# A macaron decoder layer on one core: split weights of two k tiles woven in SBUF in the first feed-forward chunk of both layers

## The chip, the core and the metric

The kernel runs on one core of a Trainium2 chip. Its time is the device time of one execution in microseconds, as the median of several; three runs of the kernel before gave 2042.21 us (2042.13 to 2042.24). One more execution was taken by the hardware profiler, and every row below comes from that one. Matmuls run on TensorE (PE, with its weight loads as PEld), the rounding of weights on ScalarE (ACT), the subtractions on VectorE (DVE), and the loads are issued by SyncE (SP).

## The reference

Everything is float32, x is 256 x 2048. A SwiGLU feed-forward layer stands before and after a block of two token mixers:

```python
x = x + 0.5 * swiglu(rmsnorm(x, ffn1_norm[l]), ffn1_w_gate[l], ffn1_w_up[l], ffn1_w_down[l])
...                      # dilated attention and forgetting attention, merged by two gates
x = x + 0.5 * swiglu(rmsnorm(x, ffn2_norm[l]), ffn2_w_gate[l], ffn2_w_up[l], ffn2_w_down[l])
return rmsnorm(x, final_norm)

def swiglu(x, w_gate, w_up, w_down):
    return (jax.nn.silu(x @ w_gate) * (x @ w_up)) @ w_down
```

`w_gate` and `w_up` are 2048 x 5632, `w_down` is 5632 x 2048. "Both layers" in this text are the two feed-forward layers.

## The kernel before

**Products in three matmuls.** Each factor of a product is split into a rounded high part (type fp32r) and a rest, the low part, that is rounded too. A product is hi x hi + hi x lo + lo x hi, three matmuls into one PSUM bank. The tokens (x transposed, `xT_hi`, `xT_lo`) are the stationary operand of 128 x 128, the weights are the moving operand of 128 x 512.

**Slabs.** Weights come in loads of 1 MB: four k tiles of 128 rows by 512 columns, in one of the four slots of `raw`. A slab is half a load, two k tiles. ACT rounds a slab (`round_slab`, one instruction of 128 x 1024 elements) into `w_hi` or `more_hi`; DVE subtracts that from the raw half (`split_slab`, one instruction of the same size) and puts the rest into `w_lo` or `more_lo`; then PE multiplies it. `w_hi` and `w_lo` hold slots 0 to 3 of a ring of six in the feed-forward layers, `more_hi` and `more_lo` slots 4 and 5. In a slot k tile 0 has the first 512 columns, k tile 1 the next 512.

**A first chunk.** The 5632 hidden columns are worked in 11 chunks of 512. The first chunk of each layer is written out: 16 slabs, 8 of the gate weights (offsets 0 to 7), then 8 of the up weights (offsets 8 to 15). A slab is multiplied by `slab`, called by `wide`: for both k tiles (j) and both halves of the tokens (t) three matmuls, twelve in all. In layer 1 slabs 0 to 3 are multiplied by `first_wide` instead. The ten chunks that follow use a scheme of seven products per block (`product`) and are not concerned. Before and in the first chunk x is still being transposed, scaled (`scale_tokens` on DVE, or on ACT in layer 1) and split (`round_x`, `split_x`) chunk by chunk; PE waits for a chunk of x ahead of every even slab.

**What orders the work.** The program of every engine is written out in order. ACT waits for the load (`raw_landed`) and, once the ring is full, for PE to be done with the slab that held the slot (`slab_done`). DVE waits for ACT (`hi_ready`), PE for DVE (`lo_ready`). SP loads into a slot of `raw` when DVE has subtracted the slab that was there (`lo_ready`). DVE has other work between its splits: sums of token pairs (`sum_pairs`, `split_pairs`) for the chunks that follow, the scaling of x and the mean for the norm.

The central lines of `slab` are 765 to 767, in `round_slab` 1343, in `split_slab` 1749; 1356 and 1788 are the same steps for the chunks that follow.

Of the kernel before, what the change touches and what calls it, by code (L numbers as in the profile page):

```python
# [19 lines left out]
F32 = mybir.dt.float32  # L20
F32R = mybir.dt.float32r
BF16 = mybir.dt.bfloat16
ALU = mybir.AluOpType
ACT = mybir.ActivationFunctionType
# [4 lines left out]
TT = SEQ // P  # L29
# [23 lines left out]
WIDE, HALF_W, DOWN = 8, 4, 8  # L53

FIRST, STEP = 2 * WIDE, 33
# [43 lines left out]
FFN_START = (0, FFN2)  # L99
# [74 lines left out]
class Place:  # L174
# [13 lines left out]
    def slab(self, offset):  # L188
        n = self.start + offset
        return n if self.i is None else self.i * self.per + n  # L190
# [11 lines left out]
def mix_place(start, per=0, i=None):  # L202
    return Place(start, FFN_LOADS + (DIL_LOADS + (start - MERGE) // 2 if start >= MERGE else 0), per, per // 2, i)


def dil_place(c):
    return Place(MIX + D_FIRST[c], FFN_LOADS + c * D_LOADS)


def dil_slab(e):  # L210

    c = max(c for c in range(D_PAIRS) if D_FIRST[c] <= e)
    r = e - D_FIRST[c]
    for s, (first, group, loads) in enumerate(D_SEVEN[c]):
        if first <= r < first + PAIR_SLABS:
            return c, r, ("paired", s, r - first)
    for first, group, l in D_GATE[c] + D_UP[c]:
        if first <= r < first + 2:
            return c, r, ("direct", l, r - first)
# [25 lines left out]
def build(nc, x, ffn1_norm, ffn1_w_gate, ffn1_w_up, ffn1_w_down, mix_norm, w_in, b_forget,  # L245
# [127 lines left out]
    ps = nc.alloc_psum_tensor("ps", [P, 8, CH], F32)  # L373
# [11 lines left out]
    def slot_hi(place, offset):  # L385
        s = place.slot(offset)
        return w_hi[:, s] if s < MIX_RING else more_hi[:, s - MIX_RING]

    def slot_lo(place, offset):
        s = place.slot(offset)  # L390
        return w_lo[:, s] if s < MIX_RING else more_lo[:, s - MIX_RING]

    def raw_half(place, offset):
        return raw[:, offset // 2 % LOADS, offset % 2 * 2:offset % 2 * 2 + 2, :]

# [53 lines left out]
    def sem(name):  # L449
        return nc.alloc_semaphore(name)  # L450
# [33 lines left out]
    hi_ready = sem("hi_ready")  # L484
    lo_ready = sem("lo_ready")
    slab_done = sem("slab_done")
# [92 lines left out]
    def fox_turn(c, r):  # L579

        if F_PAIR <= c < D_PAIRS - 1 and r in FOX_Q_TURNS:
            return c, 0, FOX_Q_TURNS.index(r)
        if F_PAIR < c and r in FOX_K_TURNS:
            return c - 1, 1, FOX_K_TURNS.index(r)
        return None
# [9 lines left out]
    with block:  # L595
# [133 lines left out]
        def tokens(t):  # L729
            return slice(t * P, (t + 1) * P)  # L730
# [21 lines left out]
        def _(pe):  # L752
# [4 lines left out]
            def slab(place, offset, banks, lhs, k0, first, last):  # L757

                hi_w, lo_w = slot_hi(place, offset), slot_lo(place, offset)
                pe.wait_ge(lo_ready, place.slab(offset + 1))  # L760
                for j in range(2):
                    for t in range(TT):
                        hi, lo = lhs(k0 + j, t)
                        acc = ps[:, banks[t], :]
                        nc.tensor.matmul(acc, hi, hi_w[:, j], start=first and j == 0, stop=False)  # L765
                        nc.tensor.matmul(acc, hi, lo_w[:, j], start=False, stop=False)  # L766
                        done = nc.tensor.matmul(acc, lo, hi_w[:, j], start=False,  # L767
                                                stop=last and j == 1)
                done.then_inc(slab_done, 1)

            def product(place, offset, bank, lhs, first, last):
# [8 lines left out]
                    done = nc.tensor.matmul(acc, lo, hi_w[:, j], start=False, stop=last and j == 1)  # L780
                done.then_inc(slab_done, 1)

            def of_x(k, t):
                return xT_hi[:, k, tokens(t)], xT_lo[:, k, tokens(t)]

# [5 lines left out]

            def wide(place, offset, banks, o):

                slab(place, offset + o, (banks, banks + 1), of_x, 2 * o, o == 0, o == WIDE - 1)

            def wide_all(place, offset, banks):
                for o in range(WIDE):
                    wide(place, offset, banks, o)
# [114 lines left out]
            def paired(place, pair):  # L913

                def of_pair(s):
                    return lambda j: (pair_hi[:, s, 2 * pair + j], pair_lo[:, s, 2 * pair + j])

                def of_tile(odd, t):
                    return lambda j: of_x(CT * PAIR_GROUPS[pair] + 2 * j + odd, t)

                for o, (bank, lhs) in enumerate((
                        (M7, of_pair(S3)), (M1, of_tile(0, 0)), (M5, of_pair(S1)), (M6, of_pair(S2)),
                        (UP0, of_pair(S4)), (GATE + 1, of_tile(1, 1)), (GATE, of_tile(1, 0)))):
                    yield o
                    product(place, PAIR_AT[pair] + o, bank, lhs, pair == 0, pair == PAIRS - 1)

            def ffn(f, b):
                silu = f * FF_CHUNKS * TT

                def step(place, i, last):  # L930
# [18 lines left out]
                    for o in range(2):  # L949
                        slab(place, DIRECT_AT + o, (GATE, GATE + 1), of_x, CT * DIRECT_GROUP + 2 * o,  # L950
                             False, False)
# [276 lines left out]
            place = mix_place(MERGE)  # L1228
# [96 lines left out]
        def _(act):  # L1325
# [5 lines left out]
            def round_slab(place, offset):  # L1331

                if place.start == 0 and offset == 0:
                    act.wait_ge(first_half_landed, 16)
                elif offset % 2 == 0 or place.start == 0 and offset == 1:
                    act.wait_ge(raw_landed[offset // 2 % LOADS], place.landed(offset // 2))
                n = place.start + offset
                if place.origin <= n < place.origin + MIX_RING and n >= MIX:

                    act.wait_ge(slab_done, n - (5 if place.origin == MIX else MIX_RING - 1))  # L1340
                elif n >= place.origin + place.ring:
                    act.wait_ge(slab_done, place.slab(offset - place.ring + 1))
                nc.scalar.activation(slot_hi(place, offset), raw_half(place, offset),
                                     ACT.Copy).then_inc(hi_ready, 1)

            def round_step(place, offset, count):

# [267 lines left out]
            for e in range(D_TOTAL):  # L1615
                round_dil(e + MIX_RING)
                c, r, _ = dil_slab(e)
                place = dil_place(c)
# [20 lines left out]
                if fox_turn(c, r) is not None:  # L1639
                    pair, part, t = fox_turn(c, r)  # L1640
# [36 lines left out]
            place = mix_place(MERGE)  # L1677
# [60 lines left out]
        def _(dve):  # L1738
# [7 lines left out]

            def split_slab(place, offset):
                dve.wait_ge(hi_ready, place.slab(offset + 1))
                nc.vector.tensor_tensor(slot_lo(place, offset), raw_half(place, offset),
                                        slot_hi(place, offset).bitcast(F32), ALU.subtract).then_inc(lo_ready, 1)  # L1750

            def weight_sum(place, q, pair, which, count):

# [418 lines left out]
            for e in range(D_TOTAL):  # L2172
                c, r, _ = dil_slab(e)
                place, merged, last = dil_place(c), c * D_COMBINED, D_SEVEN[c][-1][0]
# [175 lines left out]
            place = mix_place(MERGE)  # L2350
# [126 lines left out]
```

## Time and profile before

| what | value |
|---|---|
| median of 3 runs | 2042.21 us (2042.13 to 2042.24) |
| profiled execution: span from first to last instruction | 2040.2 us |
| PE busy | 2027.8 us (99%), 9204 matmuls |
| weight loads (PEld) busy | 1678.7 us (82%) |
| DVE busy | 1858.9 us (91%) |
| ACT busy | 1267.5 us (62%) |
| read from HBM | 400.13 MB, 197 GB/s over the span |

The span leaves out what lies before the first and after the last instruction; the profiled execution has no time of its own beside it in the results, and its span is 2.0 us below the median of the runs. Matmuls are pipelined: a matmul of 389 ns in a row overlaps the next one, so the distance of two starts tells its cost. Busy shares of ACT and DVE are those of engines that work beside PE.

### The profile page before, as it was taken

How to read it: one execution, taken by the hardware profiler on the slowest of the kernel's cores; microseconds unless marked ns; L12 is line 12 of the kernel's file. 1: busy time of each engine (PE TensorE's matmuls, PEld its weight loads, DVE VectorE, ACT ScalarE, POOL GpSimd, SP SyncE). 2: the span in 40 equal slices, each digit the busy share in tenths (PEclk: the TensorE clock that was granted, in tenths of full speed). 3: DMA queues.
4: the chain of work that ended last, by engine and by line, in shares of the span. 5: the costliest groups of instructions: out<-in, count | busy, mean ns of one | idle time of the engine just before them, and what ended most of it. 6: DMA issues, size and time to landing. Idle time of an engine off the chain costs nothing.

```text
span 2040.2 us, 26364 instructions
## 1 busy us (share of the span) xinstructions
PE 2027.8 (99%) x9204; PEld 1678.7 (82%) x9204; DVE 1858.9 (91%) x1897; ACT 1267.5 (62%) x1474; POOL 87.6 (4%) x80
## 2 busy tenths in 40 slices
PE   9999999999999999999999999999999999999998
PEld 7888888888888888888888888888888888888886
DVE  7999999999999798887689999799999999999997
ACT  7666666666666556666556556466666666666664
POOL 0000000000000000000000000000000000000000
PEclk9999999999999999999999999999999999999999
DMA  8578777787877455554536575655878777877773
GB/s 301 206 211 259 230 236 246 227 236 227 246 247 235 157 186 183 198 177 157 183 134 227 189 243 182 211 186 192 242 223 250 244 232 211 260 225 240 247 231 127
DMA packets 222143, 441.03 MB, mean 216 GB/s; under 512 B 7648, under 2 KB 7824, under 8 KB 221936
## 3 DMA queue, kind: packets, MB, share of 16 engines
q1 hardware_dynamic: 202112, 401.64, 56.1%
q0 software_dynamic: 19744, 38.28, 11.3%
q8 instruction: 47, 0.77, 0.1%
q14 instruction: 32, 0.26, 0.0%
q10 hardware_dynamic: 208, 0.08, 0.0%
HBM read 400.13 MB, written 2.10 MB: 197 GB/s over the span
## 4 chain that ended last, share of the span: by engine, by line
PE 98%; DVE 1%; ACT 0%; DMA 0%; issue 0%; SPq 0%; ACTq 0%; DVEq 0%
PE ps L765 16%; PE ps L767 16%; PE ps L766 16%; PE ps L778 12%; PE ps L780 12%; PE ps L779 12%; PE ps L1002 2%; PE ps L1003 2%; PE ps L1001 2%; PE ps L1050 2%; PE ps L1052 2%; PE ps L1051 2%; PE ps L856 1%; PE ps L834 0%; DMA xres<-in_x 0%; PE ps L1169 0%
## 5 line engine op out<-in xcount | busy, mean ns | idle before, releaser
L1788 DVE TENSOR_TENSOR w_lo<-raw,w_hi 128x1024 fp32r<-128x1024 f32 x280 | 337.9, 1219 | 7.2 <-ACT w_hi L1356 4.9
L1356 ACT ACTIVATE w_hi<-raw 128x1024 fp32r<-128x1024 f32 x280 | 290.8, 1053 | 72.6 <-PE ps L767 54.0
L1356 ACT ACTIVATE w_hi<-sums 128x1024 fp32r<-128x1024 f32 x160 | 169.8, 1063 | 204.8 <-PE ps L767 71.4
L1788 DVE TENSOR_TENSOR w_lo<-sums,w_hi 128x1024 fp32r<-128x1024 f32 x160 | 195.3, 1222 | 33.8 <-ACT w_hi L1356 31.1
L765 PE MATMUL ps<-w_hi,hT_hi 128*128 128x512 f32 x536 | 208.8, 390 | 0.0
L767 PE MATMUL ps<-w_hi,hT_lo 128*128 128x512 f32 x536 | 208.5, 389 | 0.0
L766 PE MATMUL ps<-w_lo,hT_hi 128*128 128x512 f32 x536 | 208.5, 389 | 0.0
L1788 DVE TENSOR_TENSOR more_lo<-raw,more_hi 128x1024 fp32r<-128x1024 f32 x140 | 169.2, 1219 | 6.6 <-ACT more_hi L1356 5.6
L765 PE MATMUL ps<-w_hi,xT_hi 128*128 128x512 f32 x424 | 170.1, 401 | 0.0
L1356 ACT ACTIVATE more_hi<-raw 128x1024 fp32r<-128x1024 f32 x140 | 146.4, 1054 | 32.6 <-PE ps L767 23.8
L767 PE MATMUL ps<-w_hi,xT_lo 128*128 128x512 f32 x424 | 165.7, 391 | 0.0
L766 PE MATMUL ps<-w_lo,xT_hi 128*128 128x512 f32 x424 | 165.2, 390 | 0.0
L1734 POOL DMA_DIRECT2D xres<-gate_buf x72 | 84.9, 1179 | 1848.3 <-ACT gate_buf L1490 1803.3
L1356 ACT ACTIVATE more_hi<-sums 128x1024 fp32r<-128x1024 f32 x80 | 85.1, 1063 | 99.1 <-DVE sums L1770 24.1
L778 PE MATMUL ps<-w_hi,xT_hi 128*128 128x512 f32 x354 | 139.8, 395 | 0.0
L780 PE MATMUL ps<-w_hi,xT_lo 128*128 128x512 f32 x354 | 138.1, 390 | 0.0
L779 PE MATMUL ps<-w_lo,xT_hi 128*128 128x512 f32 x354 | 137.9, 390 | 0.0
L1675 ACT ACTIVATE w_hi<-raw 128x1024 fp32r<-128x1024 f32 x87 | 92.2, 1060 | 63.6 <-PE ps L767 51.8
L2128 DVE TENSOR_TENSOR w_lo<-raw,w_hi 128x1024 fp32r<-128x1024 f32 x85 | 102.2, 1220 | 20.2 <-ACT w_hi L1576 20.2
L1576 ACT ACTIVATE w_hi<-raw 128x1024 fp32r<-128x1024 f32 x85 | 89.1, 1057 | 47.2 <-PE ps L1052 31.0
L2317 DVE TENSOR_TENSOR w_lo<-raw,w_hi 128x1024 fp32r<-128x1024 f32 x87 | 104.8, 1220 | 14.9 <-ACT w_hi L1675 14.9
L767 PEld LDWEIGHTS ps<-w_hi,hT_lo 128*128 128x128 f32 x536 | 100.6, 188 | 20.9
(366 smaller groups left out, 5007.4 us busy)
## 6 DMA issues: line engine op xcount, KB each, us to landing
raw<-in_ffn_w_up SPq DMA_DIRECT2D x88, 1024.0 KB, 5.5
raw<-in_ffn_w_down SPq DMA_DIRECT2D x88, 1024.0 KB, 5.3
raw<-in_ffn_w_gate SPq DMA_DIRECT2D x87, 1024.0 KB, 5.4
raw<-in_w_in SPq DMA_DIRECT2D x80, 1024.0 KB, 5.0
xres<-gate_buf POOLq DMA_DIRECT2D x72, 512.0 KB, 5.5
raw<-in_w_out SPq DMA_DIRECT2D x16, 1024.0 KB, 5.1
raw<-in_w_proj_dil SPq DMA_DIRECT2D x8, 1024.0 KB, 5.5
raw<-in_w_proj_fox SPq DMA_DIRECT2D x8, 1024.0 KB, 5.2
```

The costliest lines, as they stand in the source:

```text
L765: nc.tensor.matmul(acc, hi, hi_w[:, j], start=first and j == 0, stop=False)
L766: nc.tensor.matmul(acc, hi, lo_w[:, j], start=False, stop=False)
L767: done = nc.tensor.matmul(acc, lo, hi_w[:, j], start=False, stop=last and j == 1)
L778: nc.tensor.matmul(acc, hi, hi_w[:, j], start=first and j == 0, stop=False)
L779: nc.tensor.matmul(acc, hi, lo_w[:, j], start=False, stop=False)
L780: done = nc.tensor.matmul(acc, lo, hi_w[:, j], start=False, stop=last and j == 1)
L1356: nc.scalar.activation(slot_hi(place, offset), src, ACT.Copy).then_inc(hi_ready, 1)
L1576: nc.scalar.activation(slot_hi(place, r), src, ACT.Copy).then_inc(hi_ready, 1)
L1675: nc.scalar.activation(slot_hi(place, offset), src, ACT.Copy).then_inc(hi_ready, 1)
L1788: nc.vector.tensor_tensor(slot_lo(place, offset), step_source(r)[0], slot_hi(place, offset).bitcast(F32), ALU.subtract).then_inc(lo_ready, 1)
L2128: nc.vector.tensor_tensor(slot_lo(place, r), dil_source(e)[0], slot_hi(place, r).bitcast(F32), ALU.subtract).then_inc(lo_ready, 1)
L2317: nc.vector.tensor_tensor(slot_lo(place, offset), merge_source(offset)[0], slot_hi(place, offset).bitcast(F32), ALU.subtract).then_inc(lo_ ...
```

## The change

In slabs 4 to 15 of the first chunk of each feed-forward layer the high and the low part lie woven in their slot. In slabs 4 to 7 (gate weights) column c of k tile 0 and column c of k tile 1 are neighbours, so that a k tile's columns are 8 bytes apart. In slabs 8 to 15 (up weights) 16 columns of k tile 0, 64 bytes, are followed by 16 columns of k tile 1. ACT writes the high part in this order, DVE reads it and writes the low part in this order, and the matmuls take their k tile out of it with steps. The raw weights lie as before. For the up slabs the PSUM bank is written as 32 runs of 16 columns that follow one another. Slots, semaphores, the order of instructions and their number stay as they are; slabs 0 to 3 stay unwoven.

```diff
+    def is_woven(place, offset):
+        return place.start in FFN_START and place.i is None and 4 <= offset < FIRST
+
+    def woven(part, offset):
+
+        flat = part.rearrange("p a b -> p (a b)")
+        if offset < WIDE:
+            return flat.rearrange("p (c j) -> p j c", j=2)
+        return flat.rearrange("p (m j c) -> p j m c", j=2, c=16)
+
+    def as_woven(part, offset):
+
+        if offset < WIDE:
+            return part
+        return part.rearrange("p j (m c) -> p j m c", c=16)
+
+    def bank_woven(acc, offset):
+        return acc if offset < WIDE else acc.rearrange("p (m c) -> p m c", c=16)
...
+            def woven_slab(place, offset, banks, o):
+
+                pe.wait_ge(lo_ready, place.slab(offset + 1))
+                hi_w, lo_w = woven(slot_hi(place, offset), offset), woven(slot_lo(place, offset), offset)
+                for j in range(2):
+                    for t in range(TT):
+                        hi, lo = of_x(2 * o + j, t)
+                        acc = bank_woven(ps[:, banks + t, :], offset)
+                        nc.tensor.matmul(acc, hi, hi_w[:, j], start=o == 0 and j == 0, stop=False)
+                        nc.tensor.matmul(acc, hi, lo_w[:, j], start=False, stop=False)
+                        done = nc.tensor.matmul(acc, lo, hi_w[:, j], start=False, stop=o == WIDE - 1 and j == 1)
+                done.then_inc(slab_done, 1)
...
             def wide(place, offset, banks, o):
 
-                slab(place, offset + o, (banks, banks + 1), of_x, 2 * o, o == 0, o == WIDE - 1)
+                if is_woven(place, offset + o):
+                    woven_slab(place, offset + o, banks, o)
+                else:
+                    slab(place, offset + o, (banks, banks + 1), of_x, 2 * o, o == 0, o == WIDE - 1)
...
-                nc.scalar.activation(slot_hi(place, offset), raw_half(place, offset),
-                                     ACT.Copy).then_inc(hi_ready, 1)
+                hi, src = slot_hi(place, offset), raw_half(place, offset)
+                if is_woven(place, offset):
+                    hi, src = woven(hi, offset), as_woven(src, offset)
+                nc.scalar.activation(hi, src, ACT.Copy).then_inc(hi_ready, 1)
...
-                nc.vector.tensor_tensor(slot_lo(place, offset), raw_half(place, offset),
-                                        slot_hi(place, offset).bitcast(F32), ALU.subtract).then_inc(lo_ready, 1)
+                hi, lo, src = slot_hi(place, offset), slot_lo(place, offset), raw_half(place, offset)
+                if is_woven(place, offset):
+                    hi, lo, src = woven(hi, offset), woven(lo, offset), as_woven(src, offset)
+                nc.vector.tensor_tensor(lo, src, hi.bitcast(F32), ALU.subtract).then_inc(lo_ready, 1)
```

## Rows read from the trace of the kernel before

**Rows 1.** The page: span, PE's busy time, and the chain by engine.

```profile
span 2040.2 us, 26364 instructions
...
PE 2027.8 (99%) x9204; PEld 1678.7 (82%) x9204; DVE 1858.9 (91%) x1897; ACT 1267.5 (62%) x1474; POOL 87.6 (4%) x80
...
PE 98%; DVE 1%; ACT 0%; DMA 0%; issue 0%; SPq 0%; ACTq 0%; DVEq 0%
```

**Rows 2.** Timeline of PE, layer 1, slab 4 and 5: start us, us, instruction.

```profile
23.07 0.39 PE L765 MATMUL ps<-more_hi,xT_hi 128*128 128x512 f32 x1
23.30 0.39 PE L766 MATMUL ps<-more_lo,xT_hi 128*128 128x512 f32 x1
...
25.79 0.39 PE L765 MATMUL ps<-more_hi,xT_hi 128*128 128x512 f32 x1
```

**Rows 3.** Timeline of PE, layer 2: first matmuls of slabs 4, 5 and 6.

```profile
1354.93 0.39 PE L765 MATMUL ps<-more_hi,xT_hi 128*128 128x512 f32 x1
...
1357.65 0.39 PE L765 MATMUL ps<-more_hi,xT_hi 128*128 128x512 f32 x1
...
1360.38 0.39 PE L765 MATMUL ps<-w_hi,xT_hi 128*128 128x512 f32 x1
```

**Rows 4.** Busy time by stretch (us), clock granted, DMA; layer 1 twice, then layer 2.

```profile
core 0: us, PE busy (x) PEld busy (x) DVE busy (x) ACT busy (x) POOL busy (x), PEclk, DMA share, GB/s
23.07:33.95 10.88, 10.88 (x49) 9.01 (x48) 9.47 (x12) 10.59 (x20) 0.00 (x0) 1.00 1.05 386
33.95:55.70 21.75, 21.75 (x97) 18.02 (x96) 20.23 (x28) 17.59 (x25) 0.00 (x0) 1.00 0.51 177
...
1343.20:1387.50 44.30, 44.30 (x201) 36.76 (x200) 42.03 (x55) 28.23 (x36) 0.00 (x0) 1.00 0.50 173
```

**Rows 5.** Timeline of PE, matmuls of 256 columns with rounded operands, 13 in turn.

```profile
703.33 0.28 PE L1206 MATMUL ps<-xT_lo,f_both 128*16 128x256 f32 x1
...
704.70 0.28 PE L1206 MATMUL ps<-xT_lo,f_both 128*16 128x256 f32 x1
```

**Rows 6.** Groups on PE, unrounded operands: count, busy us, mean ns.

```profile
L1169 PE MATMUL ps<-probsT,v_sb 128*128 128x256 f32 x32 | 9.5, 377 | 0.0
...
L1171 PE MATMUL ps<-probsT,v_sb 128*128 128x128 f32 x32 | 6.1, 274 | 0.0
```

**Rows 7.** Groups on ACT: the rounding, and shorter and broken outputs.

```profile
L1343 ACT ACTIVATE w_hi<-raw 128x1024 fp32r<-128x1024 f32 x68 | 70.6, 1058 | 39.0 <-PE ps L767 26.6 <-PE ps L1052 6.1 <-DMA raw<-in_ffn_w_gate 6.0
...
L1380 ACT ACTIVATE xT_hi<-hidden 128x512 fp32r<-128x512 f32 x12 | 7.3, 638 | 8.6 <-DVE hidden L1817 8.6
...
L1498 ACT ACTIVATE f_both<-f_raw 128x128 fp32r<-128x128 f32 x1 | 0.3, 312 | 0.0
```

**Rows 8.** Groups on DVE: the split of a slab, and shorter and broken outputs.

```profile
L1788 DVE TENSOR_TENSOR w_lo<-raw,w_hi 128x1024 fp32r<-128x1024 f32 x280 | 337.9, 1219 | 7.2 <-ACT w_hi L1356 4.9
...
L1749 DVE TENSOR_TENSOR w_lo<-raw,w_hi 128x1024 fp32r<-128x1024 f32 x68 | 82.4, 1224 | 28.6 <-ACT w_hi L1343 28.0
...
L1817 DVE TENSOR_TENSOR hidden<-ps,gains 128x512 f32<-128x512 f32 x10 | 6.4, 682 | 1.1 <-PE ps L834 1.1
...
L2086 DVE TENSOR_TENSOR gate_buf<-rope_a,rope_b 128x128 f32<-128x128 f32 x4 | 1.2, 293 | 0.1
```

**Rows 9.** Timelines of ACT, then DVE, layer 1, slabs 4 and 5.

```profile
19.57 2.05 ACT L1343 ACTIVATE more_hi<-raw 128x1024 fp32r<-128x1024 f32 x2
...
20.70 2.36 DVE L1749 TENSOR_TENSOR more_lo<-raw,more_hi 128x1024 fp32r<-128x1024 f32 x2
```

**Rows 10.** Timeline of DVE, layer 2: slabs 4 and 5, and what follows slab 7.

```profile
1350.27 2.36 DVE L1749 TENSOR_TENSOR more_lo<-raw,more_hi 128x1024 fp32r<-128x1024 f32 x2 [0.76 <-ACT more_hi L1343]
...
1354.82 0.42 DVE L1797 TENSOR_TENSOR pair_sums<-partial 128x256 f32<-128x256 f32 x1
...
1357.91 1.29 DVE L1824 TENSOR_TENSOR xT_lo<-partial,xT_hi 128x512 fp32r<-128x512 f32 x2
```

## The prediction

> **What bounds the kernel now.** I read the page first, then the table of stretches, then the PE timeline in the chunk that changes. On the page TensorE is busy 2027.8 of 2040.2 us and the chain of waits lies on PE for 98% of the span [rows 1]. That alone does not say that the array is at its limit, since matmul ends are modelled. So I look at starts. In the first layer the first of the twelve matmuls of slab 4 starts at 23.07 us and the first of slab 5 at 25.79 us: 2.72 us for twelve, 226.7 ns from start to start [rows 2]. In the second layer slab 4 starts at 1354.93, slab 5 at 1357.65, slab 6 at 1360.38: the same 2.72 us [rows 3]. PE is without a gap in all three stretches of the two first chunks, and the granted clock is 1.00 in them [rows 4], the level of 2.4 GHz. So in the two first chunks a slab costs what its twelve matmuls cost, and nothing else shows.
>
> One detail matters. At 2.4 GHz 512 columns are 213.3 ns; the step is 226.7 ns, 0.443 ns a column against 0.417. Is the rest a fixed cost of an instruction? The 256-column matmuls with rounded operands answer that: from 703.33 to 704.70 us are 12 steps, 114.2 ns each, 0.446 ns a column [rows 5]. The loss is proportional to the columns, so something that works column by column sets a pace slightly below the array's. Both groups read four-byte elements in one unbroken run. I take that pace as a sign that the moving operand's read is what these matmuls are bound by. This is an inference, no row shows the read itself.
>
> **The change, part by part.** Counts are the same: no instruction, wait, semaphore or DMA is added, dropped or reordered. What differs is where 12 of the 16 slabs of each first chunk lie inside their slot, 24 slabs and 288 matmuls in all. Slabs 4 to 7 put column c of one k tile beside column c of the other: the matmul's moving operand steps 8 bytes per element. Slabs 8 to 15 alternate runs of 16 columns (64 bytes) of the two k tiles.
>
> *(a) Matmuls of the by-column slabs*: 4 slabs x 12 x 2 layers = 96, all on the path, since PE has no gap there. No row has a moving operand that steps over every second element. Lower bound: the unbroken form, 226.7 ns, cost 0. A gain could only be the column-proportional loss, 226.7 - 213.3 = 13.3 ns each, 1.3 us for 96. Upper bounds by the nearest rows: the unrounded f32 matmuls last 377 ns at 256 columns and 274 at 128 [rows 6], 0.80 ns a column by the difference, nearly double the rounded ones, so a half-rate feed exists in this kernel; 512 columns at that pace are 412 ns. If the read is the bound and half of what it brings is for the other k tile, each matmul takes twice its step, 453.3 ns. I take that, since the step of rows 2 and 5 is the row it is nearest to: 96 x (453.3 - 226.7) = **+21.8 us** (96 x 185 = 17.8 us with the 412 ns). Nothing hides it.
>
> Against this speaks a rule of the Trainium skill. "SBUF — State Buffer", section "Door 1: The DMA port swizzle", says that SBUF works in 16-byte lines and that two hits in a line are enough for full bandwidth. Two columns of ours lie in one line, so by this rule (a) costs nothing and the sum would be 0; with the doubled step it is 21.8 us. No row here shows a stepped moving read; the column-proportional loss is why I lean against the rule for an engine that takes 2.26 elements per ns.
>
> *(b) Matmuls of the 16-column slabs*: 8 x 12 x 2 = 192. A run of 64 bytes is read whole, so I take 0. The PSUM side is addressed in 32 runs of 16, but these follow one another, so the addresses are the old ones. Bounds: a gain of 192 x 13.3 ns = 2.6 us; a loss of one four-column read (4 x 0.443 = 1.77 ns) at each of 32 breaks, 57 ns a matmul, 10.9 us; at worst the doubled step, 192 x 226.7 ns = 43.5 us. I take 0 because nothing read is thrown away.
>
> *(c) ScalarE's rounding, `w_hi<-raw`*: 24 instructions of 1.06 us [rows 7], writing with 8-byte steps (8 of them) or in 16-column runs (16). The nearest row is `f_both<-f_raw`, which writes 128 elements in runs of 8 with gaps in 312 ns [rows 7]; from 638 ns for 512 and 1058 ns for 1024 elements an unbroken 128 would be some 325 ns [rows 7]. Short runs cost nothing, so 16-column runs are 0. Single elements have no row: between 0 and a doubling, 1 us each. I take 0.
>
> *(d) VectorE's subtraction, `w_lo<-raw,w_hi`*: 24 of 1.22 us; one input and the output are woven. Rows 8 have rope's addition, which writes 128 elements in runs of 16, at 293 ns; from 682 and 1219 ns for 512 and 1024 unbroken ones 128 would be about 280 ns [rows 8]. The 16-column runs are again nearly free. For single elements: 0 to a doubling, I take 0.
>
> What (c) and (d) cost the end if the cover is thin: in layer 1 ACT rounds slabs 4 and 5 from 19.57, DVE subtracts from 20.70 for 2.36 us (slab 4 ends near 21.9), and PE wants slab 4 at 23.07 [rows 2, 9]. The lead is 1.2 us. In layer 2 slab 4 has over 3 us of lead (DVE starts at 1350.27 [rows 10], PE at 1354.93). But queued behind slabs 4 to 7 on DVE are the sums of pairs and the scaling of x's last chunk; that chunk's low part starts at 1357.91 and lasts 1.29 us [rows 10], to 1359.2, and PE waits for it ahead of slab 6 at 1360.38 [rows 3]. Lead: 1.2 us again. With slabs 4 and 5 taking 5.44 us each on PE, 5.4 us of new slack stands ahead of slab 6, so both waits vanish, except up to 0.8 us for slab 4 in layer 1. The loads wait on `lo_ready` and have their own room: 386 GB/s around slab 4 to 7 but only 177 after [rows 4].
>
> **Sum**: 21.8 + 0 + 0 + 0 = 21.8 us on a span of 2040.2 us, so 2062.0 us of span. The profiled span is 2.0 us below the median of 2042.21 us that the runs gave; on the median the forecast is **2064.0 us**, 1.07% slower.
>
> **The rivals.**
>
> *No change (0.29).* The line is fetched once and both its elements serve, the matmul's step stays 226.7 ns: 2042.2 us. For it: 8-byte steps are small, and the loss of 6% in rows 2 and 5 may be something other than the read. Against: that loss grows with the columns. It decides if a two-element use of a line keeps up with 0.44 ns a column. This is also the result of the skill's line rule above.
>
> *The splits become the wait, the matmuls stay (0.08).* Single-element steps double ACT's and DVE's time in slabs 4 to 7. Layer 1: ACT has slab 4 at 21.5, DVE at 23.9, PE 0.8 us late; slab 6 comes at 31.0 where PE (28.5 + 0.8) wants it at 29.3, together 2.5 us. Layer 2: DVE is done with slab 7 at 1360.1 where it was at 1354.8 [rows 10], the last x chunk at 1364.5, PE 4.1 us late at slab 6. Sum 6.6 us: 2048.8 us. It decides from a delay of about 0.3 us per split on DVE (1.2 us of lead over four splits). The short runs of rows 7 and 8 speak against it, but none of them is of one element.
> A rule speaks for this rival. "Vector Engine (DVE) Microarchitecture Reference", section "5.2 Measured stream behaviour on trn2", says that a port keeps its rate only for pairs of neighbouring words, and gives 1.71 ns a column for a hopping output and 1.98 for all three streams, against 1.05. By that, an estimate, a split would take 0.7 to 1.0 us longer, and a delay of the size above would come; the steps it was measured with were longer than ours.
>
> *Every broken moving read is slow (0.12).* Both forms pay: the by-column slabs 21.8 us and the 16-column ones 10.9 us, 2074.9 us, or up to 43.5 us and 2107.5 us. For it: no matmul in this trace has a moving operand in several runs, so nothing vouches for them. Against: whole 64-byte runs.
>
> *Faster (0.01).* The column-proportional loss would have to go from all 288 matmuls: 3.8 us, 2038.4 us. Even that is under 0.2%.
>
> The forecast has 0.50: 0.45 for the doubled step, 0.05 for a part of it.
>
> **How the numbers follow.** A measurement of this kernel can tell about 0.2%, 4.1 us, from no change. Slower by over 0.2% are the forecast, the broken-read rival and most of the split rival: 0.50 + 0.12 + 0.06 = 0.68. Within it are no change, and the split rival where it is small: 0.31. Faster 0.01. The range has to take in no change and the forecast, 0.79, and the split rival between them, 0.87: from 2041.5 us to 2069 us. The upper end is the forecast plus 0.8 us for slab 4, some breaks paid in part (b), and a lower granted clock for a few matmuls should an array fed at half rate count as less busy. The likeliest case's own range is 2059 to 2069 us.
>
> **What the changed profile should show.** Starts of matmuls in slabs 4 to 7 some 450 ns apart (5.4 us a slab) and 226.7 ns from slab 8 on; `w_hi<-raw` still near 1.06 us and the split near 1.22 us in all woven slabs; no PE idle ahead of slab 6; span near 2062 us. Starts 226.7 ns apart in slabs 4 to 7 would make the forecast wrong at (a); starts further apart in slabs 8 to 15 would show (b) mis-sized; a split of 2 us or an idle PE ahead of slab 6 in layer 2 would show (d); a granted clock below 1.00 in the rows of 23 to 34 us would put a share on the clock.

## The result and the profile after

The changed kernel takes 2066.39 us (median of 4 runs, 2066.23 to 2066.45) against 2042.17 us (2042.11 to 2042.24) for the kernel before on the same chip: 24.2 us slower, a ratio of 1.0118 with a 95% interval of 1.0103 to 1.0132. The forecast was 2064.0 us in a range of 2041.5 to 2069 us.

Span and busy time on the page of the changed kernel, to be held against [rows 1]:

```profile
span 2064.6 us, 26364 instructions
...
PE 2051.6 (99%) x9204; PEld 1680.3 (81%) x9204; DVE 1860.0 (90%) x1897; ACT 1269.2 (61%) x1474; POOL 87.6 (4%) x80
```

The span grew by 24.4 us and PE's busy time by 23.8 us. DVE and ACT have 1.1 and 1.7 us more. So the time is in the matmuls. The timeline of PE in layer 1 says in which. These are the first two matmuls of slab 4 and the first ones of slabs 5, 8, 9 and 10 (start us, us, instruction):

```profile
23.24 0.61 PE L810 MATMUL ps<-more_hi,xT_hi 128*128 128x512 f32 x1
23.68 0.63 PE L811 MATMUL ps<-more_lo,xT_hi 128*128 128x512 f32 x1
...
28.66 0.64 PE L810 MATMUL ps<-more_hi,xT_hi 128*128 128x512 f32 x1
...
44.98 0.42 PE L810 MATMUL ps<-w_hi,xT_hi 128*128 128x512 f32 x1
...
47.93 0.40 PE L810 MATMUL ps<-w_hi,xT_hi 128*128 128x512 f32 x1
...
50.79 0.40 PE L810 MATMUL ps<-more_hi,xT_hi 128*128 128x512 f32 x1
```

From 23.24 to 44.98 us are the 48 matmuls of the by-column slabs: 452.9 ns each, twice the 226.7 ns of [rows 2]. The 96 matmuls from slab 8 on have a mean step of 241 ns instead of 226.7: 246 in slab 8, 238 in slab 9, 242 from slab 10 on. The stretches of the by-column slabs and of the 16-column slabs, layer 1 then layer 2 (the columns are those of [rows 4]):

```profile
23.24:44.98 21.74, 21.74 (x49) 9.93 (x48) 15.00 (x20) 14.52 (x26) 0.00 (x0) 1.00 0.76 273
44.98:68.10 23.12, 23.12 (x97) 18.07 (x96) 16.54 (x21) 14.47 (x18) 0.00 (x0) 1.00 0.29 92
1367.05:1388.79 21.74, 21.74 (x50) 9.94 (x49) 15.40 (x24) 8.10 (x9) 0.00 (x0) 1.00 0.53 184
1388.79:1411.90 23.11, 23.11 (x97) 18.06 (x96) 16.53 (x21) 11.96 (x13) 0.00 (x0) 1.00 0.29 91
```

The same instructions took 10.88 and 21.75 us in layer 1 before the change [rows 4]. In layer 2 slab 4 started at 1354.93 us [rows 3], and these are the start of slab 8 and the first matmul behind slab 15 in the kernel before, so 10.89 and 21.76 us:

```profile
1365.82 0.39 PE L765 MATMUL ps<-w_hi,xT_hi 128*128 128x512 f32 x1
...
1387.58 0.39 PE L778 MATMUL ps<-more_hi,pair_hi 128*128 128x512 f32 x1
```

With the numbers of layer 1 for both, 2 x 10.86 + 2 x 1.37 = 24.5 us, the whole difference. The granted clock is 1.00 in all four stretches. Timelines of ACT and DVE for slabs 4 and 5, beside [rows 9]:

```profile
19.73 2.23 ACT L1381 ACTIVATE more_hi<-raw 128x1024 fp32r<-128x1024 f32 x2
...
20.97 2.36 DVE L1789 TENSOR_TENSOR more_lo<-raw,more_hi 128x1024 fp32r<-128x1024 f32 x2 [0.19 <-ACT more_hi L1381]
```

The by-column split on DVE costs nothing (2.36 us for two, as before). The rounding on ACT costs 0.09 us more each (2.23 us for two, 2.05 before), and 0.05 us in slabs 6 and 7 (2.21 us for two, 2.11 before).

### The profile page after: what moved, and what is told of

Its sections match the earlier page's. It is cut to its first block, busy times and chain, and to the rows that moved or that the text cites. A ratio compares the mean times of both kernels' runs of the same rounds, so it can differ in the third digit from the quotient of the medians.

```text
span 2064.6 us, 26364 instructions
## 1 busy us (share of the span) xinstructions
PE 2051.6 (99%) x9204; PEld 1680.3 (81%) x9204; DVE 1860.0 (90%) x1897; ACT 1269.2 (61%) x1474; POOL 87.6 (4%) x80
## 4 chain that ended last, share of the span: by engine, by line
PE 98%; DVE 1%; ACT 0%; DMA 0%; issue 0%; SPq 0%; ACTq 0%; DVEq 0%
PE ps L784 14%; PE ps L786 14%; PE ps L785 14%; PE ps L797 12%; PE ps L799 12%; PE ps L798 12%; PE ps L1037 2%; PE ps L1038 2%; PE ps L1036 2%; PE ps L1087 2%; PE ps L1085 2%; PE ps L1086 1%; PE ps L811 1%; PE ps L810 1%; PE ps L812 1%; PE ps L891 1%
## 5 line engine op out<-in xcount | busy, mean ns | idle before, releaser
L1827 DVE TENSOR_TENSOR w_lo<-raw,w_hi 128x1024 fp32r<-128x1024 f32 x280 | 337.8, 1218 | 8.7 <-ACT w_hi L1393 6.3
L1393 ACT ACTIVATE more_hi<-raw 128x1024 fp32r<-128x1024 f32 x140 | 146.5, 1054 | 37.5 <-PE ps L786 23.8
L784 PE MATMUL ps<-w_hi,xT_hi 128*128 128x512 f32 x360 | 145.2, 403 | 0.0
L1393 ACT ACTIVATE more_hi<-sums 128x1024 fp32r<-128x1024 f32 x80 | 85.0, 1063 | 97.2 <-DVE sums L1809 24.2
L786 PE MATMUL ps<-w_hi,xT_lo 128*128 128x512 f32 x360 | 140.8, 391 | 0.0
L785 PE MATMUL ps<-w_lo,xT_hi 128*128 128x512 f32 x360 | 140.3, 390 | 0.0
L797 PE MATMUL ps<-w_hi,xT_hi 128*128 128x512 f32 x354 | 139.8, 395 | 0.0
L799 PE MATMUL ps<-w_hi,xT_lo 128*128 128x512 f32 x354 | 138.0, 390 | 0.0
L798 PE MATMUL ps<-w_lo,xT_hi 128*128 128x512 f32 x354 | 137.9, 390 | 0.0
L2167 DVE TENSOR_TENSOR w_lo<-raw,w_hi 128x1024 fp32r<-128x1024 f32 x85 | 102.2, 1219 | 20.2 <-ACT w_hi L1613 20.1
L1789 DVE TENSOR_TENSOR w_lo<-raw,w_hi 128x1024 fp32r<-128x1024 f32 x68 | 82.5, 1224 | 41.2 <-ACT w_hi L1381 40.6
L2356 DVE TENSOR_TENSOR w_lo<-raw,w_hi 128x1024 fp32r<-128x1024 f32 x87 | 104.7, 1220 | 14.9 <-ACT w_hi L1712 14.9
```

The lines of the kernel that those rows point to most:

```text
L1393: nc.scalar.activation(slot_hi(place, offset), src, ACT.Copy).then_inc(hi_ready, 1)
L1827: nc.vector.tensor_tensor(slot_lo(place, offset), step_source(r)[0], slot_hi(place, offset).bitcast(F32), ALU.subtract).then_inc(lo_ready, 1)
L2167: nc.vector.tensor_tensor(slot_lo(place, r), dil_source(e)[0], slot_hi(place, r).bitcast(F32), ALU.subtract).then_inc(lo_ready, 1)
L2356: nc.vector.tensor_tensor(slot_lo(place, offset), merge_source(offset)[0], slot_hi(place, offset).bitcast(F32), ALU.subtract).then_inc(lo_ ...
```

## Experiments

Seven experiments keep the arithmetic of the kernel. In the other five (the splits alone, the three sets of forms, the rival with its price) the matmuls take other columns than the product needs, so their times count and their results do not. "Step" is the distance between the starts of two matmuls, as the mean over the twelve of a slab.

**One form at a time.** The table of woven slabs is cut to one of its halves. `RUN` names the run length by slab; 1 is by column.

```diff
-        return place.start in FFN_START and place.i is None and 4 <= offset < FIRST
+        return place.start in FFN_START and place.i is None and offset in RUN
```

With `RUN = {4: 1, 5: 1, 6: 1, 7: 1}`:

> Only the by-column weaving of slabs 4 to 7 stays, slabs 8 to 15 are unwoven. If the whole cost of the by-column form is the doubled step of its 96 matmuls, the span is 2040.2 + 21.7 = 2061.9 us, the starts in slabs 4 to 7 are 453 ns apart, and slabs 8 to 15 are back at 226.7 ns (21.75 us for the eight). If part of the 2.7 us that the changed kernel loses in slabs 8 to 15 is an aftermath of the slow slabs (late splits, collisions with other engines), slabs 8 to 15 stay above 21.75 us here too, by up to 1.4 us a layer.

Measured: 2063.50 us against 2042.20 us, ratio 1.0105 (1.0088 to 1.0122), span 2061.7 us. PE, layer 1, slabs 7, 8, 9 and 10:

```profile
39.37 0.64 PE L814 MATMUL ps<-w_hi,xT_hi 128*128 128x512 f32 x1
...
44.81 0.41 PE L788 MATMUL ps<-w_hi,xT_hi 128*128 128x512 f32 x1
...
47.57 0.39 PE L788 MATMUL ps<-w_hi,xT_hi 128*128 128x512 f32 x1
...
50.29 0.39 PE L788 MATMUL ps<-more_hi,xT_hi 128*128 128x512 f32 x1
```

The step is 453.3 ns in slab 7, 230.0 in slab 8 and 226.7 from slab 9 on. The slow slabs have no aftermath but for 0.04 us in slab 8. With `RUN = {o: 16 for o in range(8, 16)}`:

> Only the 16-column weaving of slabs 8 to 15 stays, slabs 4 to 7 are unwoven. If every break in the run costs the matmul one more column time (0.443 ns, 32 breaks, 14.2 ns), each of the 192 matmuls takes 240.8 ns and the span is 2040.2 + 2.7 = 2042.9 us. If the loss was an aftermath of the slow slabs 4 to 7, the starts are 226.7 ns apart and the span is 2040.2 us.

Measured: 2044.52 us, ratio 1.0012 (1.0002 to 1.0021), span 2043.0 us, 2.8 us above the kernel before. PE, slabs 9 to 11:

```profile
37.17 0.40 PE L814 MATMUL ps<-w_hi,xT_hi 128*128 128x512 f32 x1
...
40.03 0.40 PE L814 MATMUL ps<-more_hi,xT_hi 128*128 128x512 f32 x1
...
42.93 0.40 PE L814 MATMUL ps<-more_hi,xT_hi 128*128 128x512 f32 x1
```

The step is 238.3 ns in slab 9 and 241.7 from slab 10 on. The two costs are separate and add up: the spans grew by 21.5 and 2.8 us, together 24.3 us, against 24.4 in the changed kernel.

**The ladder of run lengths.**

```diff
+    RUN = {4: 2, 5: 2, 6: 4, 7: 4, 8: 8, 9: 8, 10: 32, 11: 32, 12: 64, 13: 64, 14: 128, 15: 128}
```

> One run length per pair of slabs: 2 columns in slabs 4 and 5, 4 in 6 and 7, 8 in 8 and 9, 32 in 10 and 11, 64 in 12 and 13, 128 in 14 and 15. Theory of breaks (226.7 ns plus 0.443 ns for each of 512/run breaks): 340, 283, 255, 234, 230, 228 ns from start to start. Theory of 16-byte reads (what is fetched and not used is lost, whole 16 bytes cost nothing): 453 ns for runs of 2 columns (8 bytes of each 16), 227 ns for 4 and all longer runs. Theory that only the step between neighbouring elements counts: 227 ns for all of them. By the breaks the span is 2040.2 + 2 x 24 x (113 + 57 + 28 + 7 + 4 + 2) ns = 2050.3 us, by the 16-byte reads 2051.1 us, by the third 2040.2 us: the starts tell them apart, not the span.

Measured: 2053.78 us, ratio 1.0058 (1.0037 to 1.0078), span 2051.9 us. PE, the first matmul of slabs 4, 5, 6, 8, 10, 12 and 14 of layer 1 (each stretch between two rows is twelve steps, or twenty-four from slab 6 on):

```profile
23.01 0.61 PE L814 MATMUL ps<-more_hi,xT_hi 128*128 128x512 f32 x1
...
28.43 0.64 PE L814 MATMUL ps<-more_hi,xT_hi 128*128 128x512 f32 x1
...
33.87 0.42 PE L814 MATMUL ps<-w_hi,xT_hi 128*128 128x512 f32 x1
...
39.47 0.39 PE L814 MATMUL ps<-w_hi,xT_hi 128*128 128x512 f32 x1
...
45.06 0.40 PE L814 MATMUL ps<-more_hi,xT_hi 128*128 128x512 f32 x1
...
50.77 0.39 PE L814 MATMUL ps<-w_hi,xT_hi 128*128 128x512 f32 x1
...
56.24 0.39 PE L814 MATMUL ps<-w_hi,xT_hi 128*128 128x512 f32 x1
```

The steps, for runs of 2, 4, 8, 32, 64 and 128 columns: 453, 233, 233, 238, 228 and 226.7 ns. Runs of 2 are as slow as single columns, runs of 4 are not. That is the jump that the theory of 16-byte reads wanted, and the theory of breaks (340 ns for runs of 2, 283 for 4) is out. So is the theory of the neighbour's step, which wanted 227 ns for runs of 2. None of them had the small loss, and it does not shrink steadily with the run: 6 ns for runs of 4 and 8, 15 for 16 (the experiment before), 11 for 32, at most 2 for 64 and none for 128.

**An element per 16 bytes.**

```diff
+    RUN = {4: "far", 5: "far", 6: "far", 7: "far"}
...
+        if run == "far":
+            return flat.rearrange("p (c m j) -> p j m c", j=2, m=2)
```

> In slabs 4 to 7 neighbouring columns lie 16 bytes apart (the columns 0 to 255 and 256 to 511 of a k tile alternate too), so every element is in 16 bytes of its own; slabs 8 to 15 unwoven. If the read is paid by the 16 bytes, a matmul takes four times its step, 907 ns, and the span is 2040.2 + 96 x 0.68 = 2105.5 us. If it is paid by the broken run (one more column time per element), it stays at 453 ns and the span is 2061.9 us. ScalarE's rounding, 1.16 us by column against 1.06 unwoven, should rise further by the first theory (to about 1.9 us, one 16-byte write per element), and VectorE's split from 1.22 to about 1.9 us.

Measured: 2065.18 us, ratio 1.0113 (1.0093 to 1.0134), span 2063.3 us. The timeline of PE, the first matmuls of slabs 4, 5 and 6:

```profile
24.07 0.68 PE L814 MATMUL ps<-more_hi,xT_hi 128*128 128x512 f32 x1 [0.67 <-DVE more_lo L1793]
...
29.64 0.64 PE L814 MATMUL ps<-more_hi,xT_hi 128*128 128x512 f32 x1
...
35.17 0.64 PE L814 MATMUL ps<-w_hi,xT_hi 128*128 128x512 f32 x1
```

and those of ACT and DVE, slabs 4 and 5:

```profile
19.72 3.97 ACT L1385 ACTIVATE more_hi<-raw 128x1024 fp32r<-128x1024 f32 x2
...
21.86 4.01 DVE L1793 TENSOR_TENSOR more_lo<-raw,more_hi 128x1024 fp32r<-128x1024 f32 x2 [1.10 <-ACT more_hi L1385]
```

The matmuls stay at 461 ns, far from 907. So the price is not in bytes fetched and thrown away: with four times the 16-byte groups of an unbroken run a matmul takes 2% longer than with twice as many. ACT and DVE do slow down here, to 2.0 us each from 1.06 and 1.22. PE starts slab 4 1.0 us later than in the first experiment (24.07 against 23.07): the thin cover that the prediction had found.

**Splits woven, matmuls unbroken.**

```diff
-                if is_woven(place, offset + o):
-                    woven_slab(place, offset + o, banks, o)
-                else:
-                    slab(place, offset + o, (banks, banks + 1), of_x, 2 * o, o == 0, o == WIDE - 1)
+                slab(place, offset + o, (banks, banks + 1), of_x, 2 * o, o == 0, o == WIDE - 1)
```

> ScalarE and VectorE write slabs 4 to 15 woven as in the changed kernel, the matmuls read them unbroken (so the products of these slabs take wrong columns). Theory that the whole cost lies in the matmuls' reads: PE keeps 226.7 ns in all slabs, no wait appears, span 2040.2 us; ScalarE's by-column rounding is 1.16 us and the split 1.22 us as in the changed kernel. Theory that the woven splits would hold PE up once it isn't slow itself (the rival of the prediction): idle PE ahead of slabs 4 and 6, up to 6.6 us more.

Measured: 2042.09 us, ratio 1.0000 (0.9989 to 1.0011), span 2040.5 us, all slabs at 226.7 ns. ACT takes 2.25 us for slabs 4 and 5, DVE 2.36. The woven splits alone add nothing to the time.

**PSUM unbroken.**

```diff
-        return acc if offset < WIDE else acc.rearrange("p (m c) -> p m c", c=16)
+        return acc
```

> The changed kernel with the PSUM bank written as one unbroken row in slabs 8 to 15. If the 14 ns a matmul of the 16-column form come from PSUM in runs, slabs 8 to 15 return to 226.7 ns and the span is 2064.6 - 2.7 = 2061.9 us. If they come from the moving read in runs, nothing changes: 241 ns and 2064.6 us.

Measured: one run of 2066.46 us, span 2064.6 us, 241.7 ns in slabs 10 to 15. Nothing changes, so the loss does not come from PSUM being addressed in runs. What is left is the moving operand, the only other thing in runs.

**Twelve forms at once, first set.** The splits are unwoven; `view` takes 512 columns out of the slot. Of its forms, for instance:

```diff
+                    return {4: lambda: stepped(2), 5: lambda: stepped(3), 6: lambda: stepped(4), 7: lambda: stepped(8),
+                            8: lambda: w[:, 1:1 + CH], 9: lambda: w[:, 2:2 + CH],
+                            10: lambda: w[:, 0:16].unsqueeze(1).broadcast_to([P, 32, 16]),
+                            11: lambda: w[:, 0:1].broadcast_to([P, CH]),
...
+                        nc.tensor.matmul(acc, hi, view(hi_w, j), start=o == 0 and j == 0, stop=False)
```

> Splits unwoven, PSUM written unbroken; the matmuls of slabs 4 to 15 take 512 columns out of the slot in a form of their own per slab (the products are not those of the reference). Slab 4: step 2; 5: step 3, 256 columns twice; 6: step 4, 256 twice; 7: step 8, 128 four times; 8: unbroken from element 1; 9: unbroken from element 2; 10: the same 16 columns 32 times; 11: one element 512 times; 12: runs of 4 each 32 bytes; 13: runs of 16 each 128 bytes; 14: runs of 4 from element 2; 15: runs of 8 from element 2. Theory of the half rate (a group of four columns that fills 16 bytes passes at 0.44 ns a column, any other column costs 0.885 ns, however far the next is): 453, 453, 453, 453 ns, then 227, 227, 227, 453, 227 to 240, 227 to 240, 453, about 340 ns. Theory that every new 16 bytes cost (1.77 ns each, nothing for a second use): 453, about 680, 907, 907, 227, 227, 227, under 227 for slab 11, 227, 227, 453, 340. If the small loss of 6 to 14 ns with runs of 4 to 32 columns comes from PSUM being written in runs, slabs 12 and 13 are at 226.7 ns; if from the broken read, at 233 and 241 ns, and slab 10 tells whether a break without a hop costs too.

This program ran once, in 2071.88 us. Only its steps are read, in ns (layer 2 gives the same within 1 ns). The last two columns are what the two theories of the expectation gave.

| slab, form | step | half-rate theory | each new 16 bytes |
|---|---|---|---|
| 4, step 2 | 452 | 453 | 453 |
| 5, step 3 | 449 | 453 | 680 |
| 6, step 4 | 462 | 453 | 907 |
| 7, step 8 | 431 | 453 | 907 |
| 8, unbroken from element 1 | 238 | 227 | 227 |
| 9, unbroken from element 2 | 233 | 227 | 227 |
| 10, same 16 columns 32 times | 240 | 227 | 227 |
| 11, one element 512 times | 217 | 453 | under 227 |
| 12, runs of 4 | 233 | 227 to 240 | 227 |
| 13, runs of 16 | 241 | 227 to 240 | 227 |
| 14, runs of 4 from element 2 | 452 | 453 | 453 |
| 15, runs of 8 from element 2 | 331 | 340 | 340 |

PE, the first matmuls of slabs 7, 8, 14 and 15:

```profile
39.44 0.61 PE L830 MATMUL ps<-w_hi,xT_hi 128*128 128x512 f32 x1
...
44.61 0.42 PE L830 MATMUL ps<-w_hi,xT_hi 128*128 128x512 f32 x1
...
61.44 0.61 PE L830 MATMUL ps<-w_hi,xT_hi 128*128 128x512 f32 x1
...
66.86 0.51 PE L830 MATMUL ps<-w_hi,xT_hi 128*128 128x512 f32 x1
```

The theory of the half rate holds for slabs 4 to 7, 14 and 15: a run of 4 that straddles two groups of 16 bytes is as slow as single columns, and a run of 8 from element 2 (2 + 4 + 2) lies between. It fails for the repeated element, which is not a run of four and yet passes fastest. Slab 10 shows a loss like that of the 16-column form though it reads only the same 64 bytes again and again.

**Twelve more forms**, built the same way, to settle the question of the repeated element.

```diff
+                    def again(n):
+                        return w[:, 0:n].unsqueeze(1).broadcast_to([P, CH // n, n])
+
+                    def each(n):
+                        return w[:, 0:CH // n].unsqueeze(2).broadcast_to([P, CH // n, n])
```

> Splits unwoven, PSUM unbroken, one form of the moving operand per slab (not the reference's products). Slab 4: each element four times; 5: each element twice; 6: pairs of neighbours, each pair twice in turn; 7: runs of 6 each 32 bytes, 384 columns; 8: unbroken from element 4; 9: unbroken from element 16; 10: unbroken from element 3; 11: the same 4 columns 128 times; 12: the same 32, 16 times; 13: the same 64, 8 times; 14: the same 128, 4 times; 15: the same 256 twice. Theory that four columns in turn out of the same 16 bytes pass at full rate, whatever their order: slabs 4, 5 (two elements of 8 bytes, four columns) and 6 at 217 to 233 ns. Theory that the full rate needs an unbroken run of four from the start of 16 bytes: slabs 4, 5 and 6 at about 453 ns. Slab 7 by both: 64 x (4 x 0.443 + 2 x 0.885) = 227 ns where 384 unbroken columns would be 170. Slabs 8 and 9: 226.7 ns if only the 16 bytes matter; slab 10 like the starts at elements 1 and 2, 233 to 238. Slab 11: 217 ns like the single element; 12 to 15 fall from 238 towards 227 ns if the small loss belongs to the end of a run.

Measured (one run, 2041.93 us): slabs 4, 5 and 6 at 215.8 ns; slab 7 at 226; slabs 8, 9 and 10 at 232, 230 and 230; slab 11 at 215.8; slabs 12 to 15 at 237, 229, 226.7 and 226.7 ns. PE, the last matmul of slab 6 and the start of slabs 7 and 8:

```profile
30.76 0.38 PE L828 MATMUL ps<-w_hi,xT_lo 128*128 128x512 f32 x1
30.98 0.39 PE L826 MATMUL ps<-w_hi,xT_hi 128*128 128x384 f32 x1
...
33.69 0.40 PE L826 MATMUL ps<-w_hi,xT_hi 128*128 128x512 f32 x1
```

Pairs of neighbours read twice in turn (slab 6) are runs of 2 and still pass at full rate, because four columns in turn come from one group of 16 bytes. The need for an unbroken run of four is out. Slab 7, runs of 6 in 64 pairs of groups, is the check by number: 64 x (4 x 0.443 + 2 x 0.885) = 227 ns expected, 226 measured.

What the forms at 216 ns (slabs 4, 5, 6 and 11 here, slab 11 of the first set) have in common is that they take at least eight columns in turn out of the same 16 bytes. It is not that they read few addresses: the same 256 columns twice take 226.7 ns, the same 16 columns 32 times 240.

**Distances, PSUM and the stationary operand.** One more set of forms, in the same way. The PSUM forms, for instance:

```diff
+                    if offset == 12:
+                        return acc.rearrange("p (m j c) -> p j m c", j=2, c=4)
```

> Splits unwoven; other forms per slab, again not the reference's products. Moving read: slab 4: runs of 4 each 32 bytes; 5: runs of 4 each 64 bytes; 6: runs of 16 each 80 bytes; 7: runs of 16 each 96 bytes; 8: runs of 16 each 128 bytes; 9: runs of 32 each 144 bytes; 10: runs of 32 each 256 bytes; 13: runs of 16 each 256 bytes. Slab 11: PSUM written in runs of 2 columns that hop 16 bytes, read unbroken; 12: PSUM in runs of 4; 14: the stationary operand takes every second token, all else unbroken; 15: all unbroken. Theory that a break costs the same wherever the next run starts: equal times for slabs 6, 7, 8 and 13 (241 ns) and for 9 and 10 (238 ns). Theory that the distance counts (parts of the memory that collide): they differ, and so do 4 and 5. Slabs 11 and 12: 226.7 ns if PSUM takes runs of 2 and 4 at full rate, more if not. Slab 14: 226.7 ns if a weight load of twice its 188 ns would still fit beside the matmul or if it is not slowed, above if it is slowed and shows. Slab 15: 226.7 ns.

Measured (one run, 2044.01 us), the steps in slabs 4 to 15: 231, 228, 242, 234, 239, 237, 237, 230, 227, 242, 235 and 229 ns. Runs of 16 cost 242 ns at 80 bytes, 234 at 96, 239 at 128 and 242 at 256. The same form at 128 bytes reads 238 to 242 ns from slab 9 on in the changed kernel, so only the 234 at 96 bytes stands clearly apart: there the distance counts. PSUM in runs of 4 (slab 12) costs nothing, in runs of 2 (slab 11) at most 3 ns. A stationary operand of every second token (slab 14) costs 8 ns over the 226.7. A slab's figure can hold up to 3 ns that come from the change of form behind the slab before: slab 15, unbroken, reads 229, 232 over its first six steps and 227 over its last six.

**Better run lengths.** All 12 slabs by 8 columns, then all by 64.

```diff
+    RUN = {o: 8 for o in range(4, 16)}
```

> All 12 slabs woven by 8 columns (32 bytes). By the ladder a matmul takes 232.5 ns in place of 226.7: 288 x 5.8 ns = 1.7 us, span 2041.9 us, the median within 0.1% of the kernel before. If the ladder's low number came from its place (one pair of slabs between others) and 8 columns really cost 64 breaks of one column time, 255 ns, the span is 2040.2 + 8.2 = 2048.4 us.

Measured: 2043.85 us against 2042.13, ratio 1.0008 (0.9999 to 1.0018), span 2042.2 us, 234 ns in every slab: 288 x 7 ns = 2.0 us.

```diff
+    RUN = {o: 64 for o in range(4, 16)}
```

> All 12 slabs woven by 64 columns (256 bytes). By the ladder 227 to 229 ns a matmul: span 2040.2 to 2040.9 us, no difference from the kernel before. If the rounding or the split became slower by the hop of 512 bytes it would show in their rows (1.06 and 1.22 us), not in the span.

Measured: 2042.07 us, ratio 1.0000 (0.9990 to 1.0009), span 2040.6 us, 226.7 ns in all slabs. Weaving shows no cost at this length. No version that keeps the product is faster than the kernel before.

**The rival with its price.** The layout of an element per 16 bytes in the splits of slabs 4 to 7, matmuls unbroken.

```diff
+    RUN = {4: "far", 5: "far", 6: "far", 7: "far"}
...
-                if is_woven(place, offset + o):
-                    woven_slab(place, offset + o, banks, o)
...
+                slab(place, offset + o, (banks, banks + 1), of_x, 2 * o, o == 0, o == WIDE - 1)
```

> ScalarE and VectorE write slabs 4 to 7 with 16 bytes between neighbours (2.0 us each, as measured in the kernel with an element per 16 bytes), the matmuls read unbroken at 226.7 ns (products not the reference's). This is the prediction's rival with its price: PE late at slab 4 and slab 6 of layer 1 by 0.8 + 1.7 us and at slab 6 of layer 2 by up to 4.1 us (2.2 us if only VectorE's 0.8 us a split counts): span 2044.5 to 2046.8 us. If the splits have more room than the walk through the timelines gave, the span stays under 2042 us.

Measured: 2051.06 us, ratio 1.0044 (1.0028 to 1.0060), span 2049.3 us: 9.1 us more than the kernel before, and 2.5 us above the upper expectation. What PE waited for, in the stretch of layer 1's first chunk, then on the whole span (us in total, times, longest):

```profile
PE ps L788 <- DVE w_lo L1790: 1.0, 1, 1.0
PE ps L788 <- DVE more_lo L1790: 0.7, 1, 0.7
...
PE ps L788 <- DVE xT_lo L1864: 2.9, 1, 2.9
PE ps L801 <- DVE w_lo L1828: 1.1, 2, 0.6
```

and the clock (last column but two) around the wait of layer 2:

```profile
1360.00:1364.00 4.00, 4.00 (x19) 3.33 (x18) 3.97 (x4) 1.19 (x1) 0.00 (x0) 1.00 0.78 254
1364.00:1368.00 4.00, 1.13 (x6) 0.63 (x5) 3.58 (x8) 2.22 (x4) 0.00 (x0) 1.00 0.82 269
1368.00:1372.00 4.00, 4.00 (x13) 3.19 (x13) 4.00 (x4) 3.75 (x4) 0.00 (x0) 0.66 0.12 13
1372.00:1376.00 4.00, 4.00 (x18) 3.25 (x17) 3.90 (x7) 1.76 (x2) 0.00 (x0) 0.91 0.73 254
```

The waits of layer 1 came where the prediction's walk through the timelines put them, at slab 4 and slab 6. Layer 2's is the one on x's last chunk at slab 6. Two things had no term in the walk. Behind the 2.87 us of idle PE the granted clock fell from 2.4 to 1.2 GHz a little later, and eight unbroken matmuls took about 425 ns each (by single us from 1368 on the granted clock is 1.00, 0.64, 0.50, 0.50, 0.66 and 1.00):

```profile
1367.79 0.50 PE L788 MATMUL ps<-w_hi,xT_hi 128*128 128x512 f32 x1 [2.87 <-DVE xT_lo L1864]
...
1369.29 0.63 PE L788 MATMUL ps<-w_hi,xT_hi 128*128 128x512 f32 x1
1369.71 0.63 PE L789 MATMUL ps<-w_lo,xT_hi 128*128 128x512 f32 x1
```

That is some 8 x 200 ns = 1.6 us. And in layer 1 the delay ran on into the second chunk of hidden columns, where PE started late three times (for the first the profile names no wait, for the others it names DVE's `w_lo`):

```profile
69.75 0.50 PE L801 MATMUL ps<-w_hi,xT_hi 128*128 128x512 f32 x1
...
72.02 0.50 PE L801 MATMUL ps<-w_hi,pair_hi 128*128 128x512 f32 x1 [0.60 <-DVE w_lo L1828]
...
75.50 0.50 PE L801 MATMUL ps<-w_hi,pair_hi 128*128 128x512 f32 x1 [0.48 <-DVE w_lo L1828]
```

Held against the same matmuls of the kernel before, PE is 2.4 us late at the end of layer 1's slab 7 and 4.4 us late behind these three, by 76 us. It is still 4.4 us late when layer 2's slab 4 starts (1359.33 us, before 1354.93), and another 4.8 us are lost between slab 4 and slab 8 of layer 2. 2.4 + 2.0 + 4.8 = 9.2 us, the whole difference to within 0.1 us.

## Why the prediction was right or wrong

**(a), the by-column matmuls**: 453.3 ns taken, 452.9 measured; 21.8 us forecast, 21.7 found. The size and the place were right. The reason was not. It said that the read is the bound and half of what it brings is for the other k tile. That would give 907 ns with one element per 16 bytes, and that measured 461; a step of 8 elements measured 431. What the forms show instead: four columns in turn that come from one aligned group of 16 bytes pass at 0.42 to 0.47 ns a column (216 to 242 ns a matmul), and every other column passes alone, at 0.84 to 0.90 ns (431 to 462 ns). The doubled step of the forecast met this second rate by luck. The other row that the prediction had, the unrounded matmuls at 0.80 ns a column or 412 ns, lies near this rate too; no run shows whether it is the same limit. Nor does any run show what in the read sets the two rates.

The inference from the proportional loss of [rows 2, 5] had a true half. The forms with eight or more columns in turn out of the same 16 bytes take 216 ns, so 11 of the 13.3 ns go when the read stays that long in one group, and they do belong to the moving read. The other 2.5 ns or more were left in every form. The rule of the Trainium skill that spoke against the forecast ("SBUF — State Buffer", section "Door 1: The DMA port swizzle") says that two hits in a 16-byte line are enough for full bandwidth. The measurement differs for this operand: by column there are two, and the step doubles; it takes four. For VectorE it held (1.22 us by column, as before), for ScalarE nearly (0.05 to 0.09 us more than before).

**(b), the 16-column matmuls**: the term that was off. "I take 0 because nothing read is thrown away" was mis-sized: it measured 14 ns a matmul, 2.7 us for 192, inside the bounds of -2.6 to 10.9 us. This is the gap between the forecast span of 2062.0 us and the measured 2064.6 us. The loss belongs to the moving operand, not to PSUM (unbroken PSUM changed nothing). It is there even when the same 16 columns are read again and again (240 ns), and it varies with the length of the run and, at 96 bytes, with the distance. Why, stays open.

**(c) and (d), the splits**: 0 taken, 0 measured at the end. The row that was missing, single elements at 8 bytes, turned out like the short runs. The prediction's estimate from the Trainium skill ("Vector Engine (DVE) Microarchitecture Reference", section "5.2 Measured stream behaviour on trn2") was 0.7 to 1.0 us more per split. It did not come with steps of 8 bytes (1.22 us, nothing more); with 16 bytes it did (2.0 us, 0.8 more).

**The rivals.** No change was wrong at (a). The wait by the splits does not occur in this change, but its mechanism is real: it needs splits of 2 us, which the last experiment made, and then cost 9.1 us where the walk had 6.6. The walk counted only the waits in the first chunks, not those in the chunk behind and not the lower clock after a long wait. The rival of every broken read was half right: the 16-column form pays, at a quarter of the price it was given. The clock stayed at 1.00 with matmuls at half rate, so that share of the upper end was not needed.

## What to carry to other kernels

In all forms tried here a moving fp32r operand kept its rate, but for 0 to 7%, only if four columns in turn lay in the same aligned 16 bytes. A step of two elements, a run of two, and a run of four that straddles the boundary all doubled the matmul (452 or 453 ns), and nothing hides that when PE has no gap. If two k tiles must share memory, weave them by 64 columns (no cost seen) or 8 (3%), not by 16 (6%), and certainly not by 1 or 2 (100%). When a change slows engines beside PE, find the thinnest lead in the timelines and multiply the delay of one instruction by how many are queued before it. Follow it past the first wait as well: splits of 2 us cost 9 us through two leads of about 1.2 us, with the matmuls themselves at full rate.

## What I had not expected of the hardware

- The half rate does not get worse with distance: steps of 8, 12, 16 and 32 bytes take 452, 449, 462 and 431 ns.
- Taking eight or more columns in turn out of the same 16 bytes is faster than an unbroken read: 216 ns against 226.7 for 512 columns. So an unbroken matmul here takes 5% longer than the fastest form tried.
- Where an unbroken read starts matters a little: 226.7 ns from element 0, 238 from element 1, 233 from 2 and 232 from 4. The 230 from elements 3 and 16 are hardly more than the 229 that a slab from element 0 reads behind a change of form.
- After 2.87 us of idle PE the clock stayed at 2.4 GHz for the first 1.5 us of matmuls. Only then did it fall to 1.2 GHz, for eight matmuls, while PE was busy without a gap.
